# A kernel of two mixture-of-experts layers: the experts' rows go back to their tokens as float32 instead of as two reduced parts

## The chip, the cores and the metric

The kernel runs on one core of a Trainium2 chip. The time is device microseconds of one execution. TensorE (PE) multiplies and transposes, VectorE (DVE) and ScalarE (ACT) read PSUM and write SBUF, GpSimd (POOL) does little here, and SyncE (SP) issues nearly all transfers from HBM.

## The reference

Two layers on 256 tokens of width 2048, each a mixer (a gated recurrence in the first, sparse attention in the second) and a mixture of 16 experts, with a normalisation behind each. What the change touches is the experts' part:

```python
comb = jnp.sum(jax.nn.one_hot(e_idx, N_EXPERTS, dtype=f32) * gate[..., None], axis=-2)
hg = jnp.einsum('btd,edf->btef', x, w_gate)
hu = jnp.einsum('btd,edf->btef', x, w_up)
h = (jax.nn.silu(hg) * hu).astype(f32) * comb[..., None]
return jnp.einsum('btef,efd->btd', h.astype(x.dtype), w_down)
```

Each token goes to two experts of one group of four, so `comb` is zero for the other fourteen. Everything is float32.

## The kernel before

Tokens are sorted to experts by products with matrices of zeros and ones. An expert has 64 places (CAP). Experts are worked off in pairs, the one in partitions 0 to 63 of a PSUM bank and the other in 64 to 127, and four pairs make a group; a layer has two groups (g), so 8 pairs (x), each with the index i = 0 to 3 in its group. If an expert had more than 64 tokens, further rounds would follow; here there is one.

In `experts(lay)` of the tensor engine, `group(g, first)` runs `pair(g, i, first)` four times. A pair is:

- two transposes of its pick matrix (L1050) and the combination weights (L1052), into bank ps0; ACT copies the first to `pick_T`, DVE the second to `comb_slot`.
- for i = 0 the gather of all 16 tiles of the group's tokens (`gather_tile`, L1015 and L1016) through ps6 and ps7, emptied in turn by ACT and DVE, four tiles ahead of every fourth of the projections.
- `project` (L1035): gate into ps0 and up into ps1, eight weight steps of 2 MB, native float32 with 64 columns of weights.
- SiLU on ACT (L1550), the product with the up part and the weight on DVE (L2243), four transposes (L1078), a copy on ACT (L1552).
- the down projection (L1097), four weight steps (8 to 11), into ps2 to ps5, one bank for each chunk c of 512 of the 2048 output columns. In the last pair of a group the steps 8 and 9 give banks 2 and 3 whole, and steps 10 and 11 banks 4 and 5.

Then the rows of each chunk must go from expert order to token order and be added to the sum `acc`. This is the scatter. ACT writes `y_hi`, the rows rounded to the reduced form fp32r (`rows_hi`, L1522), DVE writes `y_lo`, the rest (`rows_lo`, L2200), each with two buffers (c % 2), and `scatter` multiplies both by `pick_T` into ps6 (tokens 0 to 127) and ps7 (128 to 255): four products for each chunk (L1024, L1025). DVE adds the two banks to `acc` (`add`, L2206). Because y_hi has two buffers, ACT waits before chunks 2 and 3 until the scatters of 0 and 1 are done (the waits on `full` in `rows_hi`). The scatters of pair x - 1 are done by the engine inside pair x: chunk 0 ahead of the projections, 1 behind the fourth weight step, 2 and 3 around the transposes (for i = 0 the two that are left behind the fourth and the eighth step). The last pair of a group scatters its own chunks 0 and 1 between the weight steps 10 and 11, and the last pair of the layer its chunks 2 and 3 at the very end, where `block_stats` (L2269) and the normalisation follow.

The weights come through six buffers of 2 MB, filled by SP in the order of use (L586, L597). SP issues a step when the engine has counted `step_used` six steps earlier. The last pair's issues are followed by those of the next stage.

Every instruction stream is written out by hand; semaphores order them.

Of the kernel before, what the change touches and what calls it, by code (L numbers as in the profile page):

```python
# [18 lines left out]
BANK = 512  # L19
# [96 lines left out]
def program(nc, a, out):  # L116
# [9 lines left out]
    with ctx:  # L126
# [9 lines left out]
        def renamed(name, words, *layers):  # L136
# [5 lines left out]
            for n, parts in enumerate(layers):  # L142
# [14 lines left out]
        ring, (w_lo, w_hi) = renamed("ring", 3 * SLOT, [("w_lo", 0, RAW * UNIT), ("w_hi", RAW * UNIT, HIGH * UNIT)])  # L157
        QK_AT, X1_AT, ATTN_AT = TT * (2 * NH * (DV + 1) + D), 8448, 13184
        ACC, H_HI, Y_HI = TT * D, 2 * TT * D, 3 * TT * D
        Y_LO, PICK8, PICK_T = Y_HI + 2 * BANK, Y_HI + 4 * BANK, Y_HI + 6 * BANK  # L160
        arena, (ws_lo0, ws_hi0, mix_lo, qn_hi, x_lo1, attn_lo, h_hi, y_hi, y_lo, pick8, pick_T) = renamed(
            "arena", 18432, [("ws_lo0", QK_AT, KT * P), ("ws_hi0", QK_AT + KT * P, KT * P)],
            [("mix_lo", QK_AT, KT * SEQ)],
            [("qn_hi", 0, TT * (2 * GQ + KVH) * DH), ("x_lo1", X1_AT, KT * SEQ), ("attn_lo", ATTN_AT, KT * SEQ)],
            [("h_hi", H_HI, TT * D), ("y_hi", Y_HI, 2 * BANK), ("y_lo", Y_LO, 2 * BANK),
             ("pick8", PICK8, TT * BANK), ("pick_T", PICK_T, 2 * SEQ)])
        WS_AT = (IH + 1) * SEQ
        arena2, (ws_lo1, ws_hi1) = renamed("arena2", 3 * SLOT, [("ws_lo1", WS_AT, KT * P), ("ws_hi1", WS_AT + KT * P, KT * P)])
# [81 lines left out]
        x_lo0 = h_lo[:, :].rearrange("p (a b) -> p a b", b=SEQ)  # L250
        h_lo = h_lo[:, :].rearrange("p (a b) -> p a b", a=TT)
        h_hi = h_hi[:, :].rearrange("p (a b) -> p a b", a=TT)
        y_hi = y_hi[:, :].rearrange("p (a b) -> p a b", a=2)
        y_lo = y_lo[:, :].rearrange("p (a b) -> p a b", a=2)
        pick8 = pick8[:, :].rearrange("p (a b) -> p a b", a=TT)
        pick_T = pick_T[:, :].rearrange("p (a b) -> p a b", a=2)
        xc_lo = hT[:, :].rearrange("p (a b) -> p a b", b=BANK)
# [10 lines left out]
        ln_gb, o = carve(arena, 0, [2, D])  # L268
        xc_hi, _ = carve(arena, 0, [KT // 2, BANK])
        acc, o = carve(arena, ACC, [TT, D])  # L270
        ln_gb2, o = carve(arena2, 0, [2, D])
        silu_g, o = carve(arena, PICK_T + 2 * SEQ, [FF])
        h_e, o = carve(arena, o, [FF])
# [146 lines left out]
        for lay in range(2):  # L420
            s = {name: sem(f"{name}_{lay}") for name in (
                "step_used", "silu_ready", "pT_full", "pT_ready", "h_ready", "hT_full", "hT_ready",
                "y_hi_ready", "y_ready", "comb_ready", "pick_ready", "ln_ready", "h_hi_ready", "h_lo_ready", "acc_ready")}
            s["loaded"] = [sem(f"expert_step_loaded_{lay}_{b}") for b in range(6)]
            s["full"] = [sem(f"tile_full_{lay}_{b}") for b in range(2)]
            s["drained"] = [sem(f"tile_drained_{lay}_{b}") for b in range(2)]
            M.append(s)
# [295 lines left out]
        def _(pe):  # L723
# [279 lines left out]
            def experts(lay):  # L1003
# [15 lines left out]
                def scatter(x, parity, c, at):  # L1019
                    pe.wait_ge(s["y_ready"], 4 * x + c + 1)  # L1020
                    for tt in range(TT):
                        pe.wait_ge(s["drained"][tt], at)
                        t, to = ps[6 + tt][:, :], pick_T[:, parity, tt * P:(tt + 1) * P]
                        nc.tensor.matmul(t, to, y_hi[:, c % 2, :], start=True, stop=False)  # L1024
                        nc.tensor.matmul(t, to, y_lo[:, c % 2, :], start=False, stop=True).then_inc(s["full"][tt], 1)  # L1025

                def project(x, i, m, bank):
                    st = 2 * m + bank
# [264 lines left out]
        def _(act):  # L1293
# [201 lines left out]
            def experts(lay):  # L1495
                s = M[lay]

                def high(c, tt):
                    act.wait_ge(s["ln_ready"], TT * c + tt + 1)
                    act.activation(h_hi[:, tt, c * BANK:(c + 1) * BANK], acc[:, tt, c * BANK:(c + 1) * BANK], ACT.Copy)\  # L1500
                       .then_inc(s["h_hi_ready"], 1)

                high(0, 0)
                act.wait_ge(logits_ready, lay + 1)
                act.activation(aff[:, :, :], logits[:, :, :], ACT.Sigmoid).then_inc(aff_ready, 1)
                high(0, 1)
                act.activation(rounds_f[:, 3:4], mhalf[:, 0:1], ACT.Silu)
                for tt in range(TT):
                    high(1, tt)

                def gathered(g, first, k):
                    act.wait_ge(s["full"][0], group_tiles(g) + gather_at(first, k // 2) + 1)
                    act.activation(xc(k), ps[6][:, :], ACT.Copy).then_inc(s["drained"][0], 1)

                def rows_hi(x, c, added=None, own=False):


                    act.wait_ge(s["step_used"], STEPS * x + (STEPS if c >= 2 or not own else STEPS - 2))
                    if c >= 2:
                        act.wait_ge(s["full"][0], added)  # L1520
                        act.wait_ge(s["full"][1], added)
                    act.activation(y_hi[:, c % 2, :], ps[2 + c][:, :], ACT.Copy).then_inc(s["y_hi_ready"], 1)  # L1522

                def pair(g, i, first):
                    x = GPAIRS * g + i
                    elder = not (first and i == 0)
                    added = [group_tiles(g) + scatter_at(first, i, c) + 1 for c in range(2)] if i > 0 else None
                    if elder and i == 0:
                        rows_hi(x - 1, 2, group_tiles(g) - 1)
                        rows_hi(x - 1, 3, group_tiles(g))  # L1530
                    if i > 0:
                        rows_hi(x - 1, 0)
                        rows_hi(x - 1, 1)
                    act.wait_ge(s["pT_full"], x + 1)
                    act.activation(pick_T[:, i % 2, :], ps[0][:, 0:SEQ], ACT.Copy).then_inc(s["pT_ready"], 1)  # L1535
                    if i == 0:
                        for k in range(0, 8, 2):
                            gathered(g, first, k)
                            if first and k % 4 == 2:
                                for tt in range(TT):  # L1540
                                    high(2 + k // 4, tt)
                    if i > 0:
                        rows_hi(x - 1, 2, added[0])
                    if i == 0:
                        for k in range(8, KT, 2):
                            gathered(g, first, k)
                    if i > 0:
                        rows_hi(x - 1, 3, added[1])
                    act.wait_ge(s["step_used"], STEPS * x + 7)
                    act.activation(silu_g[:, :], ps[0][:, :], ACT.Silu).then_inc(s["silu_ready"], 1)  # L1550
                    act.wait_ge(s["hT_full"], x + 1)
                    act.activation(hT_e[:, :, :].rearrange("p a b -> p (a b)"), ps[0][:, :], ACT.Copy).then_inc(s["hT_ready"], 1)  # L1552
                    if i == GPAIRS - 1:
                        rows_hi(x, 0, own=True)
                        rows_hi(x, 1, own=True)

                for i in range(GPAIRS):
                    pair(0, i, True)
                    if i == 0:
                        for tt in range(TT):  # L1560
                            act.wait_ge(s["h_lo_ready"], TT * 4)
                            act.activation(acc[:, tt, :], acc[:, tt, :], ACT.Copy, scale=ALPHA).then_inc(s["acc_ready"], 1)
                act.wait_ge(routed, lay + 1)
                n_r = act.value_load(rounds_i[0:1, 0:1], min_val=0, max_val=MAX_ROUNDS - 1) + 1
                with act.Fori(1, n_r * 2) as g:
                    for i in range(GPAIRS):
                        pair(g, i, False)
                for c in (2, 3):
                    rows_hi(n_r * PAIRS - 1, c, n_r * 48 - 5 + c)

            experts(0)

# [170 lines left out]
        def _(v):  # L1743
# [318 lines left out]
            def experts(lay):  # L2062
# [132 lines left out]
                    v.wait_ge(s["full"][1], group_tiles(g) + gather_at(first, k // 2) + 1)  # L2195
                    v.tensor_copy(xc(k), ps[7][:, :]).then_inc(s["drained"][1], 1)  # L2196

                def rows_lo(x, c):
                    v.wait_ge(s["y_hi_ready"], 4 * x + c + 1)
                    v.tensor_tensor(y_lo[:, c % 2, :], ps[2 + c][:, :], y_hi[:, c % 2, :].bitcast(FP32), ALU.subtract).then_inc(s["y_ready"], 1)  # L2200

                def add(c, at):
                    for tt in range(TT):
                        v.wait_ge(s["full"][tt], at + 1)
# [3 lines left out]
                def pair(g, i, first):  # L2208
# [4 lines left out]
                    for e in range(2):  # L2213
                        ins = v.tensor_copy(comb_slot[e * CAP:(e + 1) * CAP, :], ps[0][e * CAP:(e + 1) * CAP, SEQ + e:SEQ + e + 1])  # L2214
                    ins.then_inc(s["comb_ready"], 1)
                    if elder:
                        for c in ((2, 3) if i == 0 else (0, 1)):
                            rows_lo(x - 1, c)
                    if i == 0:
                        for k in range(1, 8, 2):  # L2220
                            gathered(g, first, k)
# [5 lines left out]
                        add(2, at[2])  # L2227
                    if i > 0:
                        add(0, at[0])
                        rows_lo(x - 1, 2)  # L2230
                    if i == 0:
                        for k in range(9, KT, 2):
                            gathered(g, first, k)
# [1 line left out]
                        add(3, at[3])  # L2235
                    if i > 0:
                        add(1, at[1])
                        rows_lo(x - 1, 3)
                        add(2, at[2])
                    v.wait_ge(s["step_used"], STEPS * x + 8)  # L2240
                    v.wait_ge(s["silu_ready"], x + 1)
# [4 lines left out]
                    if i > 0:  # L2246
                        add(3, at[3])
                    if i == GPAIRS - 1:
                        for c in range(2):
                            rows_lo(x, c)  # L2250
                        for c in range(2):
                            add(c, group_tiles(g) + own_at(first, c))

# [17 lines left out]

                for c in range(2):
                    block_stats(c)
                for c in (2, 3):
                    rows_lo(x, c)
                for c in (2, 3):
                    add(c, at + c)
                block_stats(2)
# [280 lines left out]
```

## Time and profile before

| | us |
|---|---|
| median of three runs | 1774.95 |
| lowest and highest | 1772.21 and 1775.88 |
| the profiled execution | 1774.51 |
| its span in the trace | 1772.7 |

| engine | busy us | instructions |
|---|---|---|
| PE | 1605.2 (91%) | 7223 |
| DVE | 720.2 (41%) | 1212 |
| ACT | 466.2 (26%) | 692 |
| POOL | 16.8 (1%) | 36 |

538.12 MB are moved, 304 GB/s in the mean. The experts of layer 0 run from about 430 to 917 us, those of layer 1 from about 1275 to 1758 us. In the page's second part the span is cut into 40 slices of 44.3 us and each digit is the busy share of a slice in tenths. In a chain or timeline a row begins with the start and the length in microseconds; square brackets give the idle time ahead of an instruction and what ended it. PEclk is the granted clock of TensorE as a share of 2.4 GHz. PE's matmuls overlap, so the length of one is longer than the distance to the next.

### The profile page before, as it was taken

Reading aid. Unit: us, or ns where it says so; the run is one execution under the profiler, and the core shown is the slowest. Engines: PE = TensorE matmul, PEld = TensorE weight load, DVE = VectorE, ACT = ScalarE, POOL = GpSimd, SP = SyncE. Lnnn points to the kernel's source line nnn. Section 1 sums busy time; section 2 is a strip of 40 time slices with the busy share of each in tenths; the row PEclk is TensorE's granted clock in tenths of the full one; section 3 lists DMA queues with packets and bytes.
Section 4 is the critical chain, followed back from the end, with each engine's and each line's share of the span. In section 5 each row is a group of like instructions: output and inputs, shape, how many; then the busy total and the mean of one; then the engine's idle time right before and its main releaser. Section 6 shows DMA issues by size and latency. Waiting matters only on the chain.

```text
span 1772.7 us, 18355 instructions
## 1 busy us (share of the span) xinstructions
PE 1605.2 (91%) x7223; PEld 953.4 (54%) x7223; DVE 720.2 (41%) x1212; ACT 466.2 (26%) x692; POOL 16.8 (1%) x36
## 2 busy tenths in 40 slices
PE   8999999998999889899879899999899988989975
PEld 6888887875433325333238778877543332533321
DVE  6675564656211121111167697655621112111116
ACT  4565535432200001000034335553220000100000
POOL 1000000000000000000000000000000000000000
PEclk9999999998999999999989899999899999989998
DMA  9666554783899999999985455549389999999995
GB/s 269 170 187 180 166 154 143 261 308 151 355 416 421 421 416 421 410 421 421 419 298 159 122 166 165 156 125 338 145 352 418 421 422 416 421 407 422 421 419 238
DMA packets 133269, 538.12 MB, mean 304 GB/s; under 512 B 19376, under 2 KB 19504, under 8 KB 86848
## 3 DMA queue, kind: packets, MB, share of 16 engines
q1 hardware_dynamic: 132608, 532.75, 79.1%
q0 software_dynamic: 576, 4.19, 0.6%
q8 instruction: 58, 0.95, 0.2%
q14 instruction: 27, 0.22, 0.0%
HBM read 534.82 MB, written 2.10 MB: 303 GB/s over the span
## 4 chain that ended last, share of the span: by engine, by line
PE 56%; issue 29%; DMA 10%; DVE 3%; ACT 1%; SPq 1%; POOL 0%; POOLq 0%; DVEq 0%; ACTq 0%
PE ps L750 12%; PE ps L752 11%; PE ps L751 11%; PE ps L1035 8%; DMA ring<-in_moe_w_down 5%; PE ps L1097 4%; DMA ring<-in_moe_w_up 4%; PE ps L731 1%; PE ps L1015 1%; PE ps L1016 1%; PE ps L1024 1%; PE ps L1207 1%; PE ps L1221 1%; PE ps L1179 0%; DMA arena<-in_x 0%
## 5 line engine op out<-in xcount | busy, mean ns | idle before, releaser
L750 PE MATMUL ps<-w_lo,x_hi 128*128 128x512 f32 x880 | 351.3, 399 | 12.8 <-DVE w_lo L1764 5.4
L1764 DVE TENSOR_TENSOR w_lo<-ring,w_hi 128x1024 fp32r<-128x1024 f32 x224 | 270.2, 1223 | 193.9 <-ACT w_hi L1314 192.4
L751 PE MATMUL ps<-w_hi,x_hi 128*128 128x512 f32 x880 | 345.4, 393 | 0.0
L1314 ACT ACTIVATE w_hi<-ring 128x1024 fp32r<-128x1024 f32 x224 | 235.5, 1058 | 314.9 <-PE ps L752 314.8
L2206 DVE TENSOR_TENSOR arena<-ps,arena 128x512 f32<-128x512 f32 x128 | 83.0, 687 | 417.7 <-PE ps L1025 417.7
L750 PEld LDWEIGHTS ps<-w_lo,x_hi 128*128 128x128 f32 x880 | 166.7, 189 | 53.2 <-issue 7.9
L751 PEld LDWEIGHTS ps<-w_hi,x_hi 128*128 128x128 f32 x880 | 166.8, 189 | 34.8 <-issue 0.5
L1035 PE MATMUL ps<-arena,hT 128*64 128x512 f32 x768 | 175.6, 612 | 8.1 <-DVE hT L2196 4.3
L1097 PE MATMUL ps<-ring,arena 128*64 128x512 f32 x768 | 170.2, 594 | 5.0 <-DMA ring<-in_moe_w_down 5.0
L1522 ACT ACTIVATE y_hi<-ps 128x512 fp32r<-128x512 f32 x64 | 36.1, 596 | 458.4 <-PE ps L1097 240.9
L752 PE MATMUL ps<-w_hi,h_lo 128*128 128x512 f32 x384 | 149.8, 390 | 0.0
L1035 PE MATMUL ps<-arena 128*64 128x512 f32 x512 | 114.9, 596 | 22.0 <-DMA arena<-in_moe_w_up 10.5
L1035 PE MATMUL ps<-ring,arena 128*64 128x512 f32 x512 | 114.5, 596 | 10.1 <-DMA ring<-in_moe_w_up 6.1
L1035 PEld LDWEIGHTS ps<-arena,hT 128*64 128x64 f32 x768 | 56.2, 142 | 118.2 <-issue 116.9
L1097 PEld LDWEIGHTS ps<-ring,arena 128*64 128x64 f32 x768 | 54.3, 137 | 116.2 <-issue 102.1
L752 PE MATMUL ps<-w_hi,x_lo 128*128 128x512 f32 x256 | 101.0, 395 | 0.0
L1035 PEld LDWEIGHTS ps<-arena 128*64 128x64 f32 x512 | 36.0, 137 | 97.8 <-issue 65.5
L2214 DVE COPY arena<-ps 64x1 f32<-64x1 f32 x32 | 5.0, 155 | 199.9 <-ACT pick_T L1535 199.7
L1024 PE MATMUL ps<-y_hi,pick_T 128*128 128x512 f32 x128 | 60.5, 473 | 28.0 <-DVE y_lo L2200 25.9
L752 PEld LDWEIGHTS ps<-w_hi,h_lo 128*128 128x128 f32 x384 | 72.3, 188 | 15.3
L1035 PEld LDWEIGHTS ps<-ring,arena 128*64 128x64 f32 x512 | 36.6, 137 | 79.8 <-issue 66.6
L1097 PE MATMUL ps<-arena 128*64 128x512 f32 x256 | 63.6, 642 | 3.2 <-ACT arena L1552 3.1
(332 smaller groups left out, 1538.3 us busy)
## 6 DMA issues: line engine op xcount, KB each, us to landing
arena<-in_moe_w_gate SPq DMA_DIRECT2D x48, 2048.0 KB, 18.4
ring<-in_moe_w_down SPq DMA_DIRECT2D x96, 1024.0 KB, 18.3
arena<-in_moe_w_up SPq DMA_DIRECT2D x32, 2048.0 KB, 20.4
ring<-in_moe_w_up SPq DMA_DIRECT2D x32, 2048.0 KB, 20.9
ring<-in_ab_w_in SPq DMA_DIRECT2D x96, 512.0 KB, 3.7
ring<-in_moe_w_gate SPq DMA_DIRECT2D x16, 2048.0 KB, 20.4
arena<-in_moe_w_down SPq DMA_DIRECT2D x32, 1024.0 KB, 18.1
ring<-in_c_w_in SPq DMA_DIRECT2D x64, 512.0 KB, 3.6
```

The source lines that it names most:

```text
L731: last = nc.tensor.transpose(t[0:m, n * P:n * P + k], src, ident[0:k, 0:k])
L750: nc.tensor.matmul(t, x_h, w_l[:, k, :], start=(opens and k == 0), stop=False)
L751: nc.tensor.matmul(t, x_h, w_h[:, k, :], start=False, stop=False)
L752: last = nc.tensor.matmul(t, x_l, w_h[:, k, :], start=False, stop=(ends_tiles(lay, n) and k == 1))
L1015: nc.tensor.matmul(t, h_hi[:, tt, mine], pick8[:, tt, :], start=(tt == 0), stop=False)
L1024: nc.tensor.matmul(t, to, y_hi[:, c % 2, :], start=True, stop=False)
L1035: last = nc.tensor.matmul(ps[bank][e * CAP:(e + 1) * CAP, :], xc(k)[:, at:at + CAP], w[:, e, kk, :], start=(k == 0), stop=(k == KT - 1), s ...
L1097: last = nc.tensor.matmul(ps[2 + 2 * half + c][e * CAP:(e + 1) * CAP, :], hT_e[:, j, e * CAP:(e + 1) * CAP], w[:, e, jj, c * BANK:(c + 1) ...
L1314: act.activation(high_unit(n), raw_unit(n)[0], ACT.Copy).then_inc(w_hi_ready, 1)
L1522: act.activation(y_hi[:, c % 2, :], ps[2 + c][:, :], ACT.Copy).then_inc(s["y_hi_ready"], 1)
L1764: v.tensor_tensor(lo, raw, high_unit(n).bitcast(FP32), ALU.subtract).then_inc(w_lo_ready, 1)
L2206: v.tensor_tensor(d, ps[6 + tt][:, :], d, ALU.add).then_inc(s["drained"][tt], 1)
```

## The change

`y_hi` and `y_lo` go; in their words lie four float32 buffers `rows_y`, one for each chunk. ACT copies a chunk once, without rounding, and signals `y_ready` itself; it no longer waits for earlier scatters and copies chunks 2 and 3 one behind the other. DVE's subtraction (`rows_lo`) goes at all its places. A scatter is two native float32 products, one for each half of the tokens, instead of four reduced ones. The additions to `acc`, the places of the scatters, the weights and their transfers stay.

```diff
@@ buffers
-        y_hi = y_hi[:, :].rearrange("p (a b) -> p a b", a=2)
-        y_lo = y_lo[:, :].rearrange("p (a b) -> p a b", a=2)
...
+        rows_y, o = carve(arena, Y_HI, [4, BANK])
@@ tensor engine, scatter
-                        nc.tensor.matmul(t, to, y_hi[:, c % 2, :], start=True, stop=False)
-                        nc.tensor.matmul(t, to, y_lo[:, c % 2, :], start=False, stop=True).then_inc(s["full"][tt], 1)
+                        nc.tensor.matmul(t, to.bitcast(FP32), rows_y[:, c, :], start=True, stop=True).then_inc(s["full"][tt], 1)
@@ scalar engine
-                def rows_hi(x, c, added=None, own=False):
+                def rows(x, c, own=False):
                     act.wait_ge(s["step_used"], STEPS * x + (STEPS if c >= 2 or not own else STEPS - 2))
-                    if c >= 2:
-                        act.wait_ge(s["full"][0], added)
-                        act.wait_ge(s["full"][1], added)
-                    act.activation(y_hi[:, c % 2, :], ps[2 + c][:, :], ACT.Copy).then_inc(s["y_hi_ready"], 1)
+                    act.activation(rows_y[:, c, :], ps[2 + c][:, :], ACT.Copy).then_inc(s["y_ready"], 1)
...
                     if i > 0:
-                        rows_hi(x - 1, 2, added[0])
+                        rows(x - 1, 2)
+                        rows(x - 1, 3)
...
-                    if i > 0:
-                        rows_hi(x - 1, 3, added[1])
@@ vector engine
-                def rows_lo(x, c):
-                    v.wait_ge(s["y_hi_ready"], 4 * x + c + 1)
-                    v.tensor_tensor(y_lo[:, c % 2, :], ps[2 + c][:, :], y_hi[:, c % 2, :].bitcast(FP32), ALU.subtract).then_inc(s["y_ready"], 1)
...
-                    if elder:
-                        for c in ((2, 3) if i == 0 else (0, 1)):
-                            rows_lo(x - 1, c)
...
-                        rows_lo(x - 1, 2)
...
-                        rows_lo(x - 1, 3)
...
-                        for c in range(2):
-                            rows_lo(x, c)
...
-                for c in (2, 3):
-                    rows_lo(x, c)
```

## Rows read from the trace of the kernel before

**Rows 1.** The page: busy time by engine, and the DMA line of the 40 slices.

```profile
PE 1605.2 (91%) x7223; PEld 953.4 (54%) x7223; DVE 720.2 (41%) x1212; ACT 466.2 (26%) x692; POOL 16.8 (1%) x36
...
DMA  9666554783899999999985455549389999999995
```

**Rows 2.** Table by stretches (start:end, length, busy of PE, PEld, DVE, ACT, POOL, PEclk, DMA share, GB/s).

```profile
500.00:520.00 20.00, 20.00 (x92) 7.04 (x92) 3.97 (x7) 1.20 (x2) 0.00 (x0) 1.00 1.01 421
560.00:580.00 20.00, 17.98 (x82) 5.81 (x80) 1.89 (x3) 0.60 (x1) 0.00 (x0) 1.00 1.01 420
720.00:740.00 20.00, 17.56 (x77) 6.42 (x75) 1.95 (x3) 1.21 (x3) 0.00 (x0) 0.91 0.96 392
728.00:732.00 4.00, 4.00 (x22) 1.46 (x20) 0.00 (x0) 0.00 (x0) 0.00 (x0) 1.00 0.75 264
1560.00:1580.00 20.00, 17.57 (x70) 6.11 (x68) 1.95 (x3) 0.60 (x1) 0.00 (x0) 0.83 0.96 392
```

**Rows 3.** Chain that ended last, end of layer 0's experts (start us, us, what).

```profile
897.85 3.65 PE ps L1097 x16
...
902.21 0.70 DVE arena L2206
...
904.28 3.61 PE ps L1097 x16
...
908.05 0.61 ACT y_hi L1522
...
908.68 0.70 DVE y_lo L2200
...
909.51 0.49 PE ps L1024
...
910.28 0.70 DVE arena L2206
```

**Rows 4.** Timeline, middle of layer 0 (start us, us, engine, line, operation, [idle before]).

```profile
657.40 3.65 PE L1097 MATMUL ps<-ring,arena 128*64 128x512 f32 x16 [0.30 <-DMA ring<-in_moe_w_down]
...
669.36 1.29 DVE L2200 TENSOR_TENSOR y_lo<-ps,y_hi 128x512 fp32r<-128x512 f32 x2
...
671.30 0.63 PE L1015 MATMUL ps<-pick,h_hi 128*128 128x512 f32 x1
...
722.08 0.75 PE L1078 MATMUL ps<-ident,arena 128*128 128x128 f32 x4 [1.57 <-DVE arena L2243]
...
723.70 5.35 PE L1097 MATMUL ps<-arena 128*64 128x512 f32 x16 [0.86 <-ACT arena L1552]
...
729.22 0.37 SPq L586 DMA_DIRECT2D arena<-in_moe_w_gate  x1
```

**Rows 5.** Groups by line and form (busy us, mean ns | idle before); one timeline row.

```profile
L1024 PE MATMUL ps<-y_hi,pick_T 128*128 128x512 f32 x128 | 60.5, 473 | 28.0 <-DVE y_lo L2200 25.9 <-DVE arena L2206 2.1
...
L1221 PE MATMUL ps<-arena 128*128 128x512 f32 x24 | 11.6, 591 | 0.0
...
1121.87 1.02 PE L1221 MATMUL ps<-arena 128*128 128x512 f32 x2
...
L1522 ACT ACTIVATE y_hi<-ps 128x512 fp32r<-128x512 f32 x64 | 36.1, 596 | 458.4 <-PE ps L1097 240.9
...
L2200 DVE TENSOR_TENSOR y_lo<-ps,y_hi x64: 678/682/693, 498.9 to 1751.9; 128x512 fp32r<-128x512 f32 x64
```

**Rows 6.** Chain that ended last, boundary of the first two pairs.

```profile
497.08 1.08 ACT y_hi L1522 x2
...
498.71 0.16 DVE arena L2214
...
498.90 0.70 DVE y_lo L2200
...
499.65 0.50 PE ps L1024
...
500.61 0.23 PE ps L1025
```

More of the change, by code:

```diff
@@ L159, in program @@
         ACC, H_HI, Y_HI = TT * D, 2 * TT * D, 3 * TT * D
-        Y_LO, PICK8, PICK_T = Y_HI + 2 * BANK, Y_HI + 4 * BANK, Y_HI + 6 * BANK
-        arena, (ws_lo0, ws_hi0, mix_lo, qn_hi, x_lo1, attn_lo, h_hi, y_hi, y_lo, pick8, pick_T) = renamed(
+        PICK8, PICK_T = Y_HI + 4 * BANK, Y_HI + 6 * BANK
+        arena, (ws_lo0, ws_hi0, mix_lo, qn_hi, x_lo1, attn_lo, h_hi, pick8, pick_T) = renamed(
             "arena", 18432, [("ws_lo0", QK_AT, KT * P), ("ws_hi0", QK_AT + KT * P, KT * P)],
@@ L164, in program @@
             [("qn_hi", 0, TT * (2 * GQ + KVH) * DH), ("x_lo1", X1_AT, KT * SEQ), ("attn_lo", ATTN_AT, KT * SEQ)],
-            [("h_hi", H_HI, TT * D), ("y_hi", Y_HI, 2 * BANK), ("y_lo", Y_LO, 2 * BANK),
+            [("h_hi", H_HI, TT * D),
              ("pick8", PICK8, TT * BANK), ("pick_T", PICK_T, 2 * SEQ)])
@@ L422, in program @@
                 "step_used", "silu_ready", "pT_full", "pT_ready", "h_ready", "hT_full", "hT_ready",
-                "y_hi_ready", "y_ready", "comb_ready", "pick_ready", "ln_ready", "h_hi_ready", "h_lo_ready", "acc_ready")}
+                "y_ready", "comb_ready", "pick_ready", "ln_ready", "h_hi_ready", "h_lo_ready", "acc_ready")}
             s["loaded"] = [sem(f"expert_step_loaded_{lay}_{b}") for b in range(6)]
@@ L1526, in pair @@
                     elder = not (first and i == 0)
-                    added = [group_tiles(g) + scatter_at(first, i, c) + 1 for c in range(2)] if i > 0 else None
                     if elder and i == 0:
-                        rows_hi(x - 1, 2, group_tiles(g) - 1)
-                        rows_hi(x - 1, 3, group_tiles(g))
+                        rows(x - 1, 2)
+                        rows(x - 1, 3)
                     if i > 0:
-                        rows_hi(x - 1, 0)
-                        rows_hi(x - 1, 1)
+                        rows(x - 1, 0)
+                        rows(x - 1, 1)
                     act.wait_ge(s["pT_full"], x + 1)
@@ L1542, in pair @@
                     if i > 0:
-                        rows_hi(x - 1, 2, added[0])
+                        rows(x - 1, 2)
+                        rows(x - 1, 3)
                     if i == 0:
@@ L1553, in pair @@
                     if i == GPAIRS - 1:
-                        rows_hi(x, 0, own=True)
-                        rows_hi(x, 1, own=True)
+                        rows(x, 0, own=True)
+                        rows(x, 1, own=True)
                 for i in range(GPAIRS):
@@ L1568, in experts @@
                 for c in (2, 3):
-                    rows_hi(n_r * PAIRS - 1, c, n_r * 48 - 5 + c)
+                    rows(n_r * PAIRS - 1, c)
             experts(0)
```

## The prediction

> **What bounds the kernel now.** I read the page first. The products' engine is busy 91% of the span, and that invites the reading that every product saved is time saved. The DMA line beneath it says otherwise: in the two expert stages (slices 12 to 20 and 32 to 39) it stands at 9 throughout [rows 1]. The change touches only those stages, so the table by stretches comes next. From 500 us on the DMA engines are occupied without a pause and move 420 to 422 GB/s, and the products' engine has room: 17.98 of 20 us busy in 560 to 580 [rows 2]. The stage is fed from HBM. A product removed there lets the engine reach its next wait for weights earlier, and nothing ends earlier. There are two exceptions for each layer. (1) Around 728 to 732 us, and again at 1560 to 1580 us, the queue ran dry: 392 instead of 421 GB/s over 20 us is 20 x (1 - 392/421) = 1.4 us of transfer lost [rows 2]. (2) Behind the last weights there is nothing left to load for the layer, and the chain of instructions runs bare. So I read the chain at the end of the layer [rows 3] and the instructions ahead of the dry spot [rows 4], and the price of one product in either form [rows 5].
>
> **Prices.** A reduced product of 512 columns follows its neighbour after 0.23 us ([rows 6], last row). Two of them behind a wait take 0.77 us until the adder starts (909.51 to 910.28 in [rows 3]), where 0.23 + 0.39 + 0.03 would be 0.65: the first one costs 0.11 us more at the head. Two that follow others take 0.46 us. The native product of the same shape, 128x128 weights and 512 columns, is in the trace at L1221 (attention): 0.591 us alone [rows 5], and two of them 1.02 us, so the second starts 1.02 - 0.59 = 0.43 us behind the first (the row at 1121.87 there). One native product for two reduced ones: 0.43 against 0.46 us of the engine, and 0.59 + 0.03 = 0.62 until the adder may start. What a native product costs at the head, behind a wait, isn't shown for this shape; it lies between nothing and the 0.11 us that the reduced one pays. I take 0.64, so 0.14 us less than now, bounds 0.05 and 0.16.
>
> The Trainium skill has a rule against this change: FP8 and Floating Point Precision, section TensorE Precision Notes, says that true FP32 takes four passes through the array. By it one native product would last 4 x 0.23 = 0.92 us, twice the pair that it replaces. The trace does not agree: 0.43 us from start to start at L1221. Nothing of the sum uses the rule; what would follow is rival B.
>
> **Part 1: y_lo and its subtraction go (64 on the vector engine, 0.68 us each [rows 5]).** That is 43.6 us of the vector engine, nearly all of it beside products. Where it is on a path:
> - Pair boundaries (i = 1 to 3, 12 in all). ACT copies from 497.08, y_lo is made at 498.90, the scatter starts at 499.65 [rows 6]; the products' engine idled 25.9 us in all behind y_lo [rows 5], 1.85 for each of the 12 boundaries and 2 ends of layers. Then the scatter could start behind the first copy, at about 497.8, and the projection would wait only for the pick and the combination column (L2214, done at 498.87). About 1.8 us each, 21 us in all. It is covered by the transfers, which run at full rate on both sides of the boundary. Without that cover it would be the largest term.
> - Group start (i = 0 of the second group). Two subtractions from 669.36 hold the vector engine for 1.29 us just when the second gathered tile wants its copy; the fourth tile therefore starts at 671.30 and its first product takes 0.63 instead of 0.40 [rows 4]. With no subtraction ahead of it the copy starts 0.3 us earlier and the head of that product (0.2 us) goes. Gain 0.35 us, bounds 0.15 and 0.4.
> - End of layer. ACT copy 908.05 to 908.66, subtraction 908.68 to 909.38, scatter 909.51 [rows 3]. Copy to scatter is 0.85 us now and would be the 0.13 of issue: 0.72 us less.
>
> **Part 2: 256 reduced products become 128 native ones.** The engine is relieved of (0.46 - 0.43) x 128 = 4 us plus heads of 0.1 us, covered except:
> - The layer's own scatters of c = 0 and 1, between the last two weight steps (901.50 to 904.28 in [rows 3]; the same in the middle of the layer). The second chunk waits for both banks to be added: products until the first addition 0.78, two additions 1.29, restart 0.05, and what is left of the 2.78 us, 0.66, is the last pair of products with its head. Then: 0.64 + 1.29 + 0.05 + 0.48 = 2.46, 0.3 us less. The step behind needs its weights: 2 MB at 421 GB/s is 5.0 us behind the landing that ends the wait at 897.85, so 902.9, still ahead of 904.0.
> - The last two scatters: twice 0.14 = 0.28 us less until the last addition.
> - Elder chunks 2 and 3 at the group start: each stands between a product and an addition that the next step waits for; 0.14 us each, 0.28.
>
> **Part 3: ACT no longer waits for the scatters of chunks 0 and 1 before it copies 2 and 3.** Each chunk has its own buffer, in the words that y_hi and y_lo held. The copy's shape stays and takes 0.6 us with float32 output (L1522, 0.596 now [rows 5]). The copies come earlier, behind them on ACT stand the gathers and the SiLU, which get no later. The buffer's reuse a pair later is ordered by the step counter; no wait is added, and no queue of DMA is moved. Worth nothing, cover: the transfers.
>
> **Sum for one layer.** End: 0.3 + 0.72 + 0.28 = 1.3 us, one for one, since in layer 0 the normalisation and the next layer's first products hang on it and in layer 1 the output does. Ahead of the dry spot: own scatters 0.3, group start 0.35, elder chunks 0.28: 0.93 us. From 657.40, where the engine last waited for weights, to the issue at 729.22 the chain is on the engines [rows 4], so that issue comes 0.93 us earlier and the dry spot shrinks from 1.4 to about 0.5 us. The transfers behind it run without a pause to the end, which so comes 0.93 us earlier. Together 2.2 us for one layer, 4.4 for two. The profiled execution took 1774.51 us (span 1772.7); less 4.4 gives 1770.1, which is 0.44 below the median of the three runs, 1774.95. As a median: 1774.95 - 4.4 = **1770.5 us**, or 0.25% less. About 0.2% (3.55 us) is what can be told from no change here.
>
> **Rivals.**
> - A. Only the bare end counts (2.6 us), or the clock eats a part. In [rows 4] the step behind the group's first turn took 5.35 us for 16 products where 3.65 is usual: the granted clock was 0.91 in that stretch [rows 2], part of it at 1.2 GHz, after idle times of 1.57 and 0.86 us, and 1.7 us went with it. Such a stretch lies just ahead of the dry spot in both layers. If it falls one step later, or once more behind the last landing, it costs 1.7 us and takes the 0.93 with it. Result 1771.0 to 1774.5. For it: the stretch is there in both layers and the change leaves those idle times. Against: the dry spot is an issue too late, and what comes before it does get shorter.
> - B, the other side. A native product takes twice as long at this place, 0.86 us. Then the adder starts 0.29 us later than now, the own scatters last 0.7 us longer (1.07 + 1.29 + 0.05 + 1.08 = 3.49), the last two 0.75 (the second bank's product is then late too): the end costs 0.7 + 0.75 - 0.72 = 0.7 us more, the middle 0.7 + 0.29 + 0.29 - 0.35 = 0.9 more, all of it added to the dry spot: 3.3 us in both layers, 1774.95 + 3.3 = 1778.3. It decides where the product costs more than 0.43 + 0.43 x 2.2/(2.2 + 1.65) = 0.68 us. Against it stands L1221 with the same shape; for it, only that L1221 has other operands and that no row shows this product here.
> - C. With the shorter group start the clock doesn't fall ahead of the dry spot. Then the issue comes over 2 us earlier, both dry spots close (2.8 us), and perhaps the half-clock stretch of the next layer's start goes too (1.7): 2.6 + 2.8 = 5.4 to 7.1 us, 1767.9 to 1769.6.
> - D. The products set the pace after all and the boundaries' 21 us and the products' 10 reach the end: about 1744 us. The DMA row speaks against it in every stretch [rows 2].
> - E. The change does nothing that can be seen: another wait (a bank, the pick) ends where y_lo's did, at the end of a layer too. 1774 to 1776. Nothing in [rows 3] stands there, the banks being long free.
>
> **How the numbers follow.** Forecast 0.46 (1769.8 to 1771.4), A 0.30, C 0.12, B 0.05, E 0.05, D 0.02. The range holds forecast, A and C nearly whole and leaves out B and D: 1767.5 to 1775.0. Faster by over 0.2% (below 1771.4): the forecast, C, D, and a small part of A less what the forecast loses at its edge, 0.57. Within 0.2%: the rest of A, E, and half of B, whose price lies at that bound, 0.37. Slower: the other half of B and what I haven't seen, 0.06.
>
> **What would show it.** The native product: second start 0.43 us behind the first, and add starts 0.62 to 0.72 us behind a scatter's start. At the boundaries no idle time ahead of the scatter, and longer waits for weights elsewhere. The 20 us around 728 at over 392 GB/s. From the last ACT copy to the scatter 0.13 us. Copies of chunks 2 and 3 back to back. The prediction is wrong if the engine's waits for weights shrink with its work, or if the dry spot stays at 1.4 us.

## The result, and the profile after

| | before | after |
|---|---|---|
| median, us | 1773.99 (8 runs) | 1781.6 (8 runs) |
| lowest and highest | 1770.81 and 1775.88 | 1778.41 and 1784.45 |
| the profiled execution | 1774.51 | 1784.45 |
| its span | 1772.7 | 1782.6 |

The ratio is 1.0043, 95% interval 1.0031 to 1.0055: 7.6 us slower, and clearly so. Forecast were 4.4 us less. The two profiled executions lie 9.9 us apart, since the one after is the slowest of its eight; the ledger below is made for those two.

The page of the changed kernel, the lines that answer to [rows 1]:

```profile
span 1782.6 us, 18203 instructions
...
PE 1640.5 (92%) x7223; PEld 948.6 (53%) x7223; DVE 685.5 (38%) x1148; ACT 463.4 (26%) x692; POOL 16.8 (1%) x36
...
DMA  9666555784899999999975455549389999999995
```

VectorE has lost 34.7 us of work; the 64 subtractions were 43.6, but the additions now run one by one and not in twos, which costs some of it. PE has not lost 4 us: its busy time has grown by 35.3, and the span by 9.9, so some 25 us of the added busy time are covered. The page's groups of instructions, which answer to [rows 5], say where the work is from:

```profile
L1023 PE MATMUL ps<-arena,pick_T 128*128 128x512 f32 x256 | 125.4, 613 | 2.0 <-ACT arena L1517 1.6
...
L1517 ACT ACTIVATE arena<-ps 128x512 f32<-128x512 f32 x64 | 35.0, 606 | 243.4 <-PE ps L1095 243.4
```

The program issues 128 scatter products. The trace has 256 instructions for them, of 0.613 us in the mean (0.592 in most cases). **One native product is two instructions of TensorE**, the second 0.43 us behind the first (four of them in 1.72 us at 894.77, in the chain at the layer's end below), so 0.86 us for each half of the tokens where two reduced products take 0.46. By these prices 128 products are 51 us more. The busy time shows 35.3; about 8 us of the difference is that the projections' own groups were busy for less, TensorE having run less at 1.2 GHz, and the rest I did not take apart. This stood in [rows 5] already: L1221 shows x24, and the code calls that product 12 times (four head groups, one product for the first 128 tokens and two for the rest). Its "two of them in 1.02 us" is one product; in the kernel before the next product starts 0.85 us behind 1121.87:

```profile
1122.72 0.49 PE L731 MATMUL ps<-ident,arena 128*128 128x128 f32 x3
```

The chain that ended last at the first pair boundary (start us, us, what), which answers to [rows 6]:

```profile
497.75 1.97 PE ps L1023 x4
499.73 13.88 PE ps L1033 x64
```

The wait for y_lo is gone: the scatter starts at 497.75 instead of 499.65. But it now takes 1.97 us, so the projections start at 499.73, 1.1 us earlier than in the kernel before (500.84), not 1.8.

The table by stretches (columns as in [rows 2]):

```profile
500.00:520.00 20.00, 20.00 (x90) 6.62 (x88) 1.84 (x3) 0.00 (x0) 0.00 (x0) 1.00 1.01 421
560.00:580.00 20.00, 18.48 (x80) 5.53 (x76) 1.38 (x2) 0.15 (x1) 0.00 (x0) 1.00 1.01 420
720.00:740.00 20.00, 17.67 (x72) 5.98 (x70) 2.04 (x3) 1.19 (x2) 0.00 (x0) 0.91 0.81 308
732.00:736.00 4.00, 4.00 (x22) 1.37 (x20) 0.00 (x0) 0.00 (x0) 0.00 (x0) 1.00 0.38 68
1560.00:1580.00 20.00, 16.69 (x71) 7.40 (x72) 3.42 (x5) 2.11 (x4) 0.00 (x0) 1.00 0.97 395
```

The transfers run at the same rate as before where they ran at full rate. The dry spot has become deep: 308 instead of 392 GB/s between 720 and 740, 68 GB/s in 732 to 736. In the timeline the transfer that ends it:

```profile
728.42 5.07 PE L1095 MATMUL ps<-arena 128*64 128x512 f32 x16 [0.89 <-ACT arena L1545]
...
733.67 0.37 SPq L585 DMA_DIRECT2D arena<-in_moe_w_gate  x1
```

It is issued at 733.67; before it was 729.22 [rows 4], 4.45 us earlier.

The chain at the end of layer 0's experts, which answers to [rows 3]:

```profile
887.01 3.65 PE ps L1033 x16
890.66 1.93 PE ps L1023 x4
...
894.77 1.72 PE ps L1023 x4
896.49 10.45 PE ps L1095 x48
906.94 3.82 PE ps L1023 x8
910.76 3.61 PE ps L1095 x16
...
914.39 0.60 ACT arena L1517
...
915.13 3.90 PE ps L1023 x8
...
919.05 0.69 DVE arena L2195
```

Before, the engine waited at 897.85 for weights and the chain began there [rows 3]. Now no weights are waited for behind the step at 887.01: scatters of 1.9 us (L1023 x4) and 3.8 (x8) stand in the chain ahead of the last three weight steps and between the last two, and the very last is 3.90 us of products without a pause, on which the additions wait.

A ledger of the two executions. The expert stage is measured from the first normalisation's `rstd` on POOL to that behind the experts: layer 0 from 497.60 us (418.57 to 916.17) to 504.26 (418.57 to 922.83), layer 1 from 497.32 to 500.64. The mixer between them has not changed (345.3 and 345.2). In the traces of the experiments the same mixer takes 341.3 to 345.6 us, so a single execution can differ by some microseconds in a part that no edit touches: the verdicts below rest on medians, and the traces say where.

| us | layer 0 | layer 1 |
|---|---|---|
| issue behind the dry spot, later by (from the stage's start) | 4.45 | 1.0 |
| the rest, at the layer's end | 2.2 | 2.3 |
| stage longer by | 6.7 | 3.3 |

In layer 0 the last weight steps lag by the same 4.46 us as the issue at 733.67 (887.01 against 882.55 for the last step of the projections), so this term went through one for one. The end's 2.2 us are 1.0 net for the two scatters around the transposes in the last pair (they no longer fit ahead of the weights' landing), 1.0 for the own scatters (906.94 to 910.76, 3.82 instead of 2.78) and 0.2 from the start of the last step on: 0.3 more from ACT's copy to the end of the last addition, with the saved subtraction already in it, and 0.1 less ahead of the copy.

The dry spots of the two layers differ by the clock. In the first layer of the changed kernel TensorE ran at 1.2 GHz for one stretch at 642 us (16 products in 5.35 us, not 3.65) and one at 728 (16 products in 5.07 us; the kernel before lost as much there, [rows 4]). The stretch at 642, 1.7 us of the 4.45, is no fixed part of the change: of the other nine kernels traced here only the one with one reduced product has such a stretch between 640 and 660 us (granted clock 0.83 in 650 to 660), the others stand at 1.00 there, the changed kernel with the product ahead too. In the second layer the changed kernel kept 2.4 GHz at the turn, where the kernel before had lost 2.6 us by it (16 products in 6.24 us; granted clock 0.83 in the last of [rows 2]).

### The profile page after: what moved, and what is told of

The parts are those of the page before. It is cut to its first block, busy times and chain, and to the rows that moved or that the text cites. A ratio compares the mean times of both kernels' runs of the same rounds, so it can differ in the third digit from the quotient of the medians.

```text
span 1782.6 us, 18203 instructions
## 1 busy us (share of the span) xinstructions
PE 1640.5 (92%) x7223; PEld 948.6 (53%) x7223; DVE 685.5 (38%) x1148; ACT 463.4 (26%) x692; POOL 16.8 (1%) x36
## 4 chain that ended last, share of the span: by engine, by line
PE 59%; issue 29%; DMA 6%; DVE 4%; ACT 1%; POOL 0%; SPq 0%; POOLq 0%; DVEq 0%
PE ps L749 11%; PE ps L751 11%; PE ps L750 11%; PE ps L1033 9%; PE ps L1095 6%; DMA arena<-in_moe_w_up 5%; PE ps L1023 3%; PE ps L730 1%; PE ps L1014 1%; PE ps L1015 1%; PE ps L1205 1%; PE ps L1219 1%; DVE w_lo L1757 0%; DMA arena<-in_x 0%; DVE arena L2227 0%
## 5 line engine op out<-in xcount | busy, mean ns | idle before, releaser
L2195 DVE TENSOR_TENSOR arena<-ps,arena 128x512 f32<-128x512 f32 x128 | 88.6, 692 | 498.4 <-PE ps L1023 497.9
L1033 PE MATMUL ps<-arena,hT 128*64 128x512 f32 x768 | 170.9, 596 | 12.9 <-DMA arena<-in_moe_w_gate 5.2
L1033 PE MATMUL ps<-arena 128*64 128x512 f32 x512 | 116.7, 603 | 25.2 <-DMA arena<-in_moe_w_up 12.1
L1023 PE MATMUL ps<-arena,pick_T 128*128 128x512 f32 x256 | 125.4, 613 | 2.0 <-ACT arena L1517 1.6
L1543 ACT ACTIVATE arena<-ps 128x512 f32<-128x512 f32 x16 | 9.6, 597 | 369.3 <-PE ps L1033 369.3
L1517 ACT ACTIVATE arena<-ps 128x512 f32<-128x512 f32 x64 | 35.0, 606 | 243.4 <-PE ps L1095 243.4
```

The source lines that it names most:

```text
L1023: nc.tensor.matmul(t, to.bitcast(FP32), rows_y[:, c, :], start=True, stop=True).then_inc(s["full"][tt], 1)
L1033: last = nc.tensor.matmul(ps[bank][e * CAP:(e + 1) * CAP, :], xc(k)[:, at:at + CAP], w[:, e, kk, :], start=(k == 0), stop=(k == KT - 1), s ...
L1517: act.activation(rows_y[:, c, :], ps[2 + c][:, :], ACT.Copy).then_inc(s["y_ready"], 1)
L2195: v.tensor_tensor(d, ps[6 + tt][:, :], d, ALU.add).then_inc(s["drained"][tt], 1)
```

## The experiments

The reasons stood against each other as P (the loss is the engine's time for the products, where nothing covers it) and S (the new order of copies, additions and waits costs it). All ratios are to the kernel before.

**All of the new order, with cheap products.**

```diff
-        rows_y, o = carve(arena, Y_HI, [4, BANK])
+        rows_y = rows_r[:, :].rearrange("p (a b) -> p a b", a=4)      # fp32r over the same words
-                        nc.tensor.matmul(t, to.bitcast(FP32), rows_y[:, c, :], start=True, stop=True).then_inc(s["full"][tt], 1)
+                        nc.tensor.matmul(t, to, rows_y[:, c, :], start=True, stop=True).then_inc(s["full"][tt], 1)
```

> The changed kernel in all of its order (four buffers, one copy by ACT, no subtraction), but the copy is rounded to the reduced form and each half of the tokens gets one reduced product, so the low part of the experts' rows is left out. Theory P (a native product is two instructions of 0.43 us on the products' engine, and the loss is their length at the group's turn and at the layer's end): the two reduced instructions in place of four take 1.5 us off each scatter of the changed kernel, both dry spots of the transfers close (1.4 us each) and each layer's end is about 1.8 us shorter than in the kernel before: 1774.0 - 2 x 3.2 = 1767.6, ratio 0.996. Theory S (the new order of copies, additions and waits costs the time, the products being near neutral): no better than 1774, up to 1781.

Measured 1770.5 us against 1773.8, ratio 0.9980 (0.9972 to 0.9989). With the changed kernel's order and cheap products the time is 3.3 us below the kernel before, so the order isn't what costs; S has fallen. The chain at the end of layer 0:

```profile
899.00 3.65 PE ps L1095 x16
...
904.96 3.61 PE ps L1095 x16
...
908.59 0.60 ACT rows_r L1517
...
909.32 0.51 PE ps L1023
...
909.85 2.58 DVE arena L2195 x4
```

The stretches with the dry spots (columns as in [rows 2]):

```profile
720.00:740.00 20.00, 17.07 (x80) 6.51 (x78) 2.19 (x5) 2.25 (x5) 0.00 (x0) 1.00 1.01 417
1560.00:1580.00 20.00, 18.09 (x78) 6.83 (x80) 1.20 (x4) 2.82 (x6) 0.00 (x0) 0.91 1.01 418
```

From the first product behind the last wait for weights (899.00) to the last additions it goes as I had worked out: until `rstd` 16.5 us, where the kernel before takes 18.3 (897.85 to 916.17), 1.8 less. The dry spots are closed, too (417 and 418 GB/s). But that half of the expectation brought nothing: the stages are 1.4 and 2.0 us shorter, about what the ends give. The 3.3 us are not the order's alone: of the 1.8 us at layer 0's end 0.73 are the subtraction, and most of the rest comes from products that are half as long as the pair before (the own scatters take 2.31 us, 902.65 to 904.96, instead of 2.78).

**The products alone, in the old order.**

```diff
-                        nc.tensor.matmul(t, to, y_hi[:, c % 2, :], start=True, stop=False)
-                        nc.tensor.matmul(t, to, y_lo[:, c % 2, :], start=False, stop=True).then_inc(s["full"][tt], 1)
+                        nc.tensor.matmul(t, to.bitcast(FP32), y_hi[:, c % 2, :].bitcast(FP32), start=True, stop=True).then_inc(s["full"][tt], 1)
...
-                    act.activation(y_hi[:, c % 2, :], ps[2 + c][:, :], ACT.Copy).then_inc(s["y_hi_ready"], 1)
+                    act.activation(y_hi[:, c % 2, :].bitcast(FP32), ps[2 + c][:, :], ACT.Copy).then_inc(s["y_hi_ready"], 1)
```

> The kernel before with native products only: ACT stores its copy in float32, the subtraction stays with its waits (nobody reads what it writes), two buffers, and each scatter is two native products. Theory P: the layer's end gets 2.2 + 0.72 = 2.9 us longer (what the changed kernel shows there, plus the subtraction that it saved), the turn between the groups about 3: 2 x 5.9 = 11.8 us, 1786, ratio 1.0066; slower than the changed kernel. Theory S: as before, 1774, ratio 1.000.

Measured 1783.8 against 1773.8, ratio 1.0056 (1.0040 to 1.0071), 10 us. Expected were 11.8. The changed kernel's 7.6 lies between what the two parts allow: 10.0 - 3.3 = 6.7 if all of the former gain is the order's, and 10.0 - 1.5 = 8.5 if only the subtraction at the two ends is.

**Half the chunks native, in two places.** Both kernels have 32 native and 32 reduced chunks; only the pairs differ.

```diff
+        NATIVE = (0, 1)        # pairs of a group; in the second kernel (2, 3)
...
+                        if p in NATIVE:
+                            nc.tensor.matmul(t, to.bitcast(FP32), rows_y[:, c, :], start=True, stop=True).then_inc(s["full"][tt], 1)
+                            continue
...
+                    if p in NATIVE:
+                        act.activation(rows_y[:, c, :], ps[2 + c][:, :], ACT.Copy).then_inc(s["y_ready"], 1)
+                        return
...
+                    if p in NATIVE:        # vector engine: no subtraction
+                        return
```

> Native products with one float32 copy for the first two pairs of each group only (32 of the 64 chunks, scattered inside the pairs i = 1 and 2, where the transfers set the pace); the last two pairs of a group keep y_hi, y_lo and four reduced products. Theory P with the place deciding: 1773 to 1775, ratio 0.9995 to 1.0005. Theory P with the count deciding (each of the 64 costs the same): half of the change's loss, 1777.8, ratio 1.0021. Theory S: also about half.

> The other half: native products with one float32 copy for the last two pairs of each group (32 of the 64 chunks: inside the pair i = 3, its own chunks, the group's turn and the layer's end); the first two pairs keep y_hi, y_lo and four reduced products. Theory P with the place deciding: all of the change's loss, 1780 to 1782, ratio 1.0035 to 1.0045. With the count deciding: half, 1777.8, ratio 1.0021.

Measured 1774.2, ratio 1.0003 (0.9994 to 1.0012), for the covered pairs, and 1782.0, ratio 1.0045 (1.0032 to 1.0058), for the exposed ones: nothing against all of the loss. The same number of products costs 0 or 8 us by its place alone. Covered pairs, the two stretches with the dry spots:

```profile
720.00:740.00 20.00, 17.51 (x81) 6.92 (x80) 2.38 (x6) 2.60 (x6) 0.00 (x0) 1.00 1.01 414
1560.00:1580.00 20.00, 17.56 (x77) 6.38 (x75) 1.95 (x3) 0.98 (x2) 0.00 (x0) 0.91 0.94 387
```

The second is as dry as in the kernel before (387 against 392 GB/s), the first less (414).

Exposed pairs, the chain at the end of layer 0, with the same three lengths as the changed kernel (1.93, 3.82, 3.90):

```profile
888.59 1.93 PE ps L1027 x4
...
904.87 3.82 PE ps L1027 x8
...
913.05 3.90 PE ps L1027 x8
```

**Occupation without any native product.**

```diff
-                        nc.tensor.matmul(t, to, y_hi[:, c % 2, :], start=True, stop=False)
-                        nc.tensor.matmul(t, to, y_lo[:, c % 2, :], start=False, stop=True).then_inc(s["full"][tt], 1)
+                        for turn_ in range(2):
+                            nc.tensor.matmul(t, to, y_hi[:, c % 2, :], start=True, stop=False)
+                            last = nc.tensor.matmul(t, to, y_lo[:, c % 2, :], start=False, stop=True)
+                        last.then_inc(s["full"][tt], 1)
```

> The kernel before with its reduced pair of products issued twice over in each scatter, the second time from the start, so that the sum stays the same: eight reduced instructions, about 0.92 us for each half of the tokens, with every wait, copy and subtraction of before. No native product anywhere. Theory P (only the engine's time at exposed places counts, whatever fills it): like native products with the old waits, 1783 to 1787, ratio 1.005 to 1.007. If something in the native form itself costs (its operands, the float32 rows): nearer to 1774 to 1777.

Measured 1785.8 against 1774.5, ratio 1.0064 (1.0047 to 1.0081). The groups of the two products, 256 of each:

```profile
L1025 PE MATMUL ps<-y_hi,pick_T 128*128 128x512 f32 x256 | 110.0, 430 | 25.9 <-DVE y_lo L2202 25.9
L1026 PE MATMUL ps<-y_lo,pick_T 128*128 128x512 f32 x256 | 103.3, 404 | 0.0
```

Four reduced instructions for each half of the tokens, 0.92 us, cost 11 us; two native ones, 0.86 us, cost 10 with the same waits. The intervals of the two ratios overlap: a cost of the native form beside its time on the engine can't be seen.

**Is the dry spot worth closing?**

```diff
-                    if elder and i == 0:
-                        add(3, at[3])
...
                     v.scalar_tensor_tensor(h_e[:, :], ps[1][:, :], comb_slot[:, 0:1], silu_g[:, :], ALU.mult, ALU.mult).then_inc(s["h_ready"], 1)
...
-                    if i > 0:
+                    if elder:
                         add(3, at[3])
```

> The kernel before; in the first pair of a group the vector engine makes the experts' product h_e ahead of the addition of elder chunk 3 instead of behind it. That takes about 2 us off the chain ahead of the transfers' dry spot in both layers and nothing off the layer's end. If closing the dry spot is worth what it moves: 2 x 1.3 = 2.6 us less, 1771.2, ratio 0.9985. If it is given back before the last weights land, as the single-reduced kernel's first layer hints: 1773.5 to 1774, ratio 0.9995 to 1.000.

Measured 1773.1 against 1774.5, ratio 0.9994 (0.9985 to 1.0003): not to be told from no change. The interval just reaches the 0.9985 of the full gain, so that there is none rests on the traces. The stretches:

```profile
720.00:740.00 20.00, 17.20 (x80) 7.26 (x79) 3.27 (x8) 1.96 (x4) 0.00 (x0) 0.96 1.02 422
1560.00:1580.00 20.00, 17.60 (x80) 6.62 (x82) 3.50 (x8) 2.22 (x5) 0.00 (x0) 0.95 1.01 421
```

The chain at layer 0's end:

```profile
898.17 3.65 PE ps L1097 x16
...
904.60 3.61 PE ps L1097 x16
...
909.83 0.49 PE ps L1024
```

The transfers have no pause any more (422 and 421 GB/s), and yet the engine gets the weights of the last step but one at 898.17, 479.4 us behind the stage's start, as before (479.3). The stages took 497.7 and 498.3 us, before 497.6 and 497.3. A transfer that is moved away from a pause isn't thereby a transfer that lands earlier at the end.

**The same in the changed kernel.** The edit is the same.

> The changed kernel, and in the first pair of a group the vector engine makes h_e ahead of the addition of elder chunk 3, as in the kernel with the product ahead. It takes about 2.6 us off the chain of the group's turn and nothing off the layer's end. Theory P with a ledger of two terms (the dry spot that the late turn widens by 4.5 us in layer 0 and 0.9 in layer 1 of the profiled execution, and 2.2 us at each end): the first term shrinks by up to 2.6 and 0.9 us, the second stays: 1778 to 1779.5, ratio to before 1.0025 to 1.003. If the turn is as much without effect as closing the dry spot was in the kernel before: 1781.6, ratio 1.0043.

Measured 1780.7 against 1775.6, ratio 1.0029 (1.0018 to 1.0040), inside what the ledger of two terms gave. The stretches:

```profile
720.00:740.00 20.00, 19.14 (x88) 6.87 (x84) 2.13 (x3) 0.99 (x2) 0.00 (x0) 1.00 0.99 397
1560.00:1580.00 20.00, 19.14 (x88) 6.99 (x86) 2.14 (x3) 1.19 (x2) 0.00 (x0) 1.00 0.99 394
```

The dry spots are back at about what the kernel before has (392 GB/s over these 20 us are 1.4 us of transfer lost, 397 and 394 are 1.1 and 1.3), and the stages take 500.3 and 500.2 us: the difference between layers is gone, and 2.7 and 2.9 us remain over before. The intervals of this ratio and of the changed kernel's 1.0043 overlap, so the 4.4 us of layer 0 are shown by the trace of one execution only, one that had the stretch at 642 us; the medians lie 2.5 us closer to the kernel before with this edit (5.1 against 7.6).

**Shorter exposed places, exact sums.** From the results the way to a gain is plain: the end of a layer, in reduced form. Banks 0 and 1 are free when the own chunk 1 and the last chunk are scattered.

```diff
+                    if not first and i == 0:
+                        pe.wait_ge(s["drained"][0], group_tiles(g))
+                        pe.wait_ge(s["drained"][1], group_tiles(g))
...
-                                scatter(x, i % 2, c, group_tiles(g) + own_at(first, c))
+                                scatter(x, i % 2, c, group_tiles(g) + own_at(first, 0), 6 if c == 0 else 0)
...
-                    scatter(n_r * PAIRS - 1, 1, c, n_r * 48 - 4 + c)
+                    scatter(n_r * PAIRS - 1, 1, c, n_r * 48 - 2, 6 if c == 2 else 0, early=c == 2)
```

(`early` issues the two y_hi products ahead of the wait for y_lo; the vector engine's additions read the same banks; h_e goes ahead of the addition as above.)

> The kernel before with shorter exposed places and the same sums: the own chunk 1 of a group's last pair and the layer's last chunk are scattered into banks 0 and 1, which are free then, so that the engine doesn't wait for the additions; in the layer's last chunk 2 the y_hi products go ahead of the wait for y_lo; h_e goes ahead of the addition of elder chunk 3. Theory P (the exposed places count one for one): own chunks 0.85 us, last chunks 0.3 to 0.5 us less, 1.2 to 1.4 us for a layer: 1773.8 - 2.6 = 1771.2, ratio 0.9985, and 0.997 if the closed dry spot counts as well. If the end of a layer is set by something else (the last weights' landing): 1774.

Measured 1771.2 against 1774.5, ratio 0.9982 (0.9973 to 0.9991): 3.3 us less, and faster than both kernels. Timeline at the end of layer 0:

```profile
897.96 3.65 PE L1108 MATMUL ps<-ring,arena 128*64 128x512 f32 x16 [0.26 <-DMA ring<-in_moe_w_down]
...
901.54 0.50 PE L1032 MATMUL ps<-y_hi,pick_T 128*128 128x512 f32 x1
...
902.31 2.48 DVE L2217 TENSOR_TENSOR arena<-ps,arena 128x512 f32<-128x512 f32 x4 [2.65 <-PE ps L1033]
...
903.59 3.65 PE L1108 MATMUL ps<-ring,arena 128*64 128x512 f32 x16
...
908.17 0.73 PE L1024 MATMUL ps<-y_hi,pick_T 128*128 128x512 f32 x2 [0.92 <-ACT y_hi L1533]
...
909.35 2.48 DVE L2217 TENSOR_TENSOR arena<-ps,arena 128x512 f32<-128x512 f32 x4
```

The own scatters take 2.05 us (901.54 to 903.59) instead of 2.78, the additions run four in a row (L2217 x4 in 2.48 us), and from the last wait for weights to `rstd` it is 16.95 us (897.96 to 914.91) instead of 18.3: 1.4 less, as expected for one layer. In layer 1 it is also 16.95 us (1739.21 to 1756.16). The stages as wholes are 2.1 and 0.6 us shorter, because the weights of the last step but one came 0.7 us earlier in the one and 0.8 later in the other; terms below 1 us in a single trace are to be read with that in mind.

## Why the prediction was wrong

**The step that failed** is the price of one native product: "two of them 1.02 us, so the second starts 0.43 us behind the first". The two were the halves of one product. The count in [rows 5], x24, should have been held against the 12 calls in the code; the projections show the same factor (L1035: 64 calls for each of the 16 pairs, 1024, and 768 + 512 + 512 + 256 = 2048 instructions in the trace). With 0.86 us the prediction's own rival B holds, and its mechanism is what happened. I had given it 0.05, on the strength of that one row. The rule in the Trainium skill, FP8 and Floating Point Precision, section TensorE Precision Notes, that true FP32 takes several passes, pointed the right way, and my sentence that the trace does not agree with it was wrong: 0.86 us is 3.7 times the 0.23 us from one reduced product to the next. My estimate by that rule, 4 x 0.23 = 0.92 us, is 0.06 too high. The trace shows two instructions for a product; that each makes two of the four passes would fit, but no row shows passes.

**Point by point.**

- The transfers set the pace of the stage: right. 35 us of added busy time, 10 of added span; the covered pairs cost nothing.
- Part 1 (y_lo goes). The end of a layer: right to a tenth in the kernel with one reduced product, where copy to scatter is 0.73 us (908.59 to 909.32), that is 0.12 behind the copy. The boundaries: 1.1 us at the first, not 1.8, since the scatter is longer, and covered as said.
- Part 2: sign wrong. Own scatters 1.0 us more instead of 0.3 less. Last two scatters until the last addition, 3.92 us (915.13 to 919.05) instead of 2.94, the products alone setting the pace, where it was products waiting for additions before.
- A place overlooked: the scatters around the transposes in the layer's last pair. I took them as covered by the weights' landing. In the kernel before the engine waits 0.23 us there, so the cover is that thin, and about 1.0 us came through.
- The dry spot "shrinks and the transfers behind it come earlier one for one": wrong in the direction of shrinking (the kernel with the product ahead: no gain from closing it, 1.3 us in each layer), right in that of growing (the table below). So 0.93 of the 2.2 us for each layer would probably not have come even with the price that I had, and the forecast would have been rival A's 2.6 us.
- Rival B: mechanism and sign right, size short. 3.3 us were given, 7.6 measured. The overlooked scatters at the layer's end (1.0 for each layer) are about half of the 4.3 between them. Another part is that the engine came to the turn late already, by 2.8 us at the own scatters of layer 0 (663.79 against 660.99): 1.7 of these are the stretch at 1.2 GHz at 642 us, and the rest the scatters around the transposes of that pair, no longer covered. How the other 2.3 us of the median divide no run shows.

**What stays open.** Why a widened dry spot reaches the end and a closed one doesn't. That it is so, more traces than these two show. The issue behind the turn and the start of the last projection step in layer 0, both from the stage's start and against the kernel before (us, minus is earlier):

| kernel | issue | last projection step |
|---|---|---|
| changed | +4.45 | +4.46 |
| native in the exposed pairs | +2.96 | +2.67 |
| reduced pair issued twice | +1.76 | +2.44 |
| native products alone | +1.32 | +1.25 |
| changed, product ahead | -0.13 | +0.54 |
| native in the covered pairs | -1.75 | +0.02 |
| one reduced product | -1.82 | +0.36 |
| product ahead | -3.55 | +0.13 |
| two more banks | -5.00 | -0.75 |

A late issue goes through nearly whole, an early one hardly at all. In the kernel with one reduced product 276.1 MB had been moved when the last step but one was there, in the kernel before 275.5; the 0.6 MB too much are 1.4 us of transfer, about what closing won. I take them for a part of the step behind, which is issued while this one is under way; no run shows that, nor why it would share the engines with it. Also the halves of the ledger in layer 0 against layer 1 hang on where the clock fell in one execution of each kernel.

## What to carry to other kernels

- Before a row of the trace prices an operation, divide its count by the calls in the code. A mean of 0.59 us times one was the wrong price of something that is two instructions.
- An engine that is busy 91% took 11 us more for nothing in one place (the covered pairs, 1616.3 us busy instead of 1605.2), and 15 us more in another (the exposed pairs, 1620.3) made the kernel 8 us slower. Test by place: the same edit on two halves of the work, chosen by what covers them, told more here than the edit's whole.
- In a stage paced by transfers, the cover of the last steps is measured by the wait for the last weights (0.23 us here), not by the mean room of the engine.

## What the runs showed of the hardware that I had not expected

- A native float32 product of 512 columns with 128x128 weights is two TensorE instructions, 0.43 us apart, 0.86 us in all (256 for 128 products); a reduced (fp32r) one is a single instruction every 0.23 us. A sum of a high and a low reduced product is thus about half the price of the native one.
- Four reduced and two native instructions of nearly equal time (0.92 and 0.86 us) cost a program the same (11 and 10 us).
- The granted clock did not fall with the longer products: 0.971 in the mean of the profiled execution before and 0.980 after, and 0.980 to 0.984 over the eight runs after, where the fast runs before have 0.971 to 0.980. What this took off the loss no run shows by itself.
